# A two-layer transformer kernel on one core: row fetches through a ring of six buffers from the end of the first expert product on, and spills issued one at a time

## What is computed

```
def peer_ffn(h, w_q, sub_keys, u_tab, v_tab):      # cut; 16384 experts, 8 heads, 16 picks per head
    s = einsum(h @ w_q, sub_keys)                   # scores of 128 + 128 keys per head
    s_top, i_top = top_k(s, 16); best, pos = top_k(sums of pairs, 16)
    idx = ...; w = softmax(best)                    # 128 experts per position
    act = gelu(einsum('nhkd,nd->nhk', u_tab[idx], h))
    out = einsum('nhk,nhkd->nd', w * act, v_tab[idx])
```

## Time and profile before

| | |
|---|---|
| median of three runs | 3257.43 us |
| the profiled execution | 3261.52 us |
| its span | 3259.7 us |
| mean granted TensorE clock, share of full speed | 0.961 |
| busy: PE, DVE, ACT, POOL | 3080.0, 2214.2, 1151.3, 413.1 us |
| row 48 is used, row 79 is used | from 2576.11, from 2703.15 us |
| first matmul of the second product | 2707.39 us |

### The profile page before, as it was taken

How to read it: one execution, slowest core, us unless ns; L and a number is a source line. 1 busy time by engine, 2 the same in 40 slices (tenths; PEclk the granted TensorE clock), 3 DMA queues, 4 the chain that set the end, 5 groups by cost and what they waited for, 6 DMA issues and landing times.

```text
span 3259.7 us, 42988 instructions
## 1 busy us (share of the span) xinstructions
PE 3080.0 (94%) x17723; PEld 2817.2 (86%) x17723; DVE 2214.2 (68%) x3737; ACT 1151.3 (35%) x1569; POOL 413.1 (13%) x264
## 2 busy tenths in 40 slices
PE   7998998999999999999999998999999857999998
PEld 7888887878789889998878788899999857999998
DVE  6446875746644543666753579998997547899997
ACT  2234233222223432455552223444444312333332
POOL 0000000000000000000000000011111235566551
PEclk9888999999999998999999999999999978999999
DMA  5223112232232232211214414467477869999995
GB/s 227 106 97 137 44 49 103 83 104 92 84 122 73 71 142 101 78 65 66 99 64 161 181 65 177 164 217 256 169 243 261 294 223 363 402 401 401 402 401 219
DMA packets 215714, 571.10 MB, mean 175 GB/s; under 512 B 14288, under 2 KB 129488, under 8 KB 180064
## 3 DMA queue, kind: packets, MB, share of 16 engines
q1 hardware_dynamic: 176496, 426.14, 36.3%
q0 software_dynamic: 36864, 134.23, 11.0%
q10 hardware_dynamic: 2160, 7.99, 0.6%
HBM read 495.95 MB, written 72.35 MB: 174 GB/s over the span
## 4 chain that ended last, share of the span: by engine, by line
PE 78%; DVE 11%; DMA 5%; ACT 3%; SPq 2%; issue 1%; POOL 0%; DVEq 0%; ACTq 0%
PE bank L573 70%; DMA ub<-in_urow,gsel 3%; PE bank L1236 2%; DVE wl L528 2%; SPq L3046 2%; PE bank L637 1%; DMA gelu_spill<-gst 1%; DVE ub L3229 1%; PE bank L2507 1%; PE bank L585 1%; PE bank L644 1%; DVE Ah L3030 1%; ACT wh L521 1%; PE bank L2516 1%; PE bank L1501 0%
## 5 line engine op out<-in xcount | busy, mean ns | idle before, releaser
L573 PE MATMUL bank<-hh,wh 128*128 128x512 f32 (+2 forms) x2512 | 928.3, 370 | 70.6 <-DVE wl L528 60.6
L573 PE MATMUL bank<-hl,wh 128*128 128x512 f32 (+2 forms) x2512 | 902.2, 359 | 0.0
L573 PE MATMUL bank<-hh,wl 128*128 128x512 f32 (+2 forms) x2512 | 897.0, 357 | 0.0
L528 DVE TENSOR_TENSOR wl<-ring,wh 128x2048 fp32r<-128x2048 f32 (+2 forms) x249 | 554.1, 2225 | 312.6 <-ACT wh L521 311.9
L521 ACT ACTIVATE wh<-ring 128x2048 fp32r<-128x2048 f32 (+2 forms) x249 | 463.6, 1862 | 770.2 <-PE bank L573 761.6
L573 PEld LDWEIGHTS bank<-hh,wh 128*128 128x128 f32 x2512 | 487.4, 194 | 129.1 <-DVE wl L528 65.3
L573 PEld LDWEIGHTS bank<-hl,wh 128*128 128x128 f32 x2512 | 486.8, 194 | 50.4 <-issue 6.0
L573 PEld LDWEIGHTS bank<-hh,wl 128*128 128x128 f32 x2512 | 486.8, 194 | 46.4
L3215 POOL DMA_INDIRECT ub<-in_urow,gsel x128 | 193.6, 1513 | 1499.5 <-DVE gsel L2957 885.7
L573 PE MATMUL bank<-ph,wh 128*128 128x384 f32 x1024 | 346.1, 338 | 28.3 <-DVE pl L3178 28.3
L573 PE MATMUL bank<-ph,wl 128*128 128x384 f32 x1024 | 345.2, 337 | 0.0
(11 more groups left out here) (515 smaller groups left out, 4452.2 us busy)
## 6 DMA issues: line engine op xcount, KB each, us to landing
ring<-in_v SPq DMA_DIRECT2D x68, 1024.0 KB
ring<-in_u SPq DMA_DIRECT2D x64, 1024.0 KB
ring<-in_ada SPq DMA_DIRECT2D x24, 1024.0 KB
gelu_spill<-gst SPq DMA_DIRECT2D x128, 192.0 KB
weight_spill<-stage SPq DMA_DIRECT2D x24, 1024.0 KB, 11.1
gv<-gelu_spill SPq DMA_DIRECT2D x64, 384.0 KB
wv<-weight_spill SPq DMA_DIRECT2D x64, 384.0 KB
ring<-in_wup SPq DMA_DIRECT2D x22, 1024.0 KB
```

Of the source, the lines that this page charges most:

```text
L528: v.then_inc(v.e.tensor_tensor(wl[q % 2][:, 0:n], ring[k % 4][:, 0:n], wh[q % 2][:, 0:n].bitcast(F32), S_), s("parts"))
L573: ins = p.e.matmul(out, l, r, start=start and i == 0, stop=stop and i == len(pairs) - 1, skip_group_check=not check)
```

## The change

The ring. Rows 0 to 47 use the two buffers as before. From row `RT` = 48 on there are six: `ub2` to `ub5`, which now lie in the place of `x3` (over `stage0`), and the old two. Fetch 48 waits for the last spill of `stage0` (block 4), fetch n from 52 on waits until row n-6 is used. `ub6` and `ub7` are gone. The read of the residual into `x3` waits until all 256 rows are used. How many rows stand where does not change.

The spills. The four spills of a block are issued singly: those of the first block of a `hot(j)` at q = 16, 18, 20 and 22 of the same `hot(j)`; those of the second block in the first four steps of the next one; those of the last block (5) beside rows 48 to 51 (`rows_sy`).

```
         sb("ub_kept", [128, 2048], F32, ar)
         ph = [...]; pl = [...]
+        with ExitStack() as a2:
+            ub += [sb(f"ub{j}", [128, 1024], F32, a2) for j in range(2, 6)]
         x3 = sb("x3", [128, 8, 512], F32, ar)
         acc = sb("acc", [128, 1024], F32, ar)
         gwt = sb("gwt", [128, 128], F32, ar)
-        with ExitStack() as a2:
-            ub += [sb(f"ub{j}", [128, 1024], F32, a2) for j in range(2, 8)]
...
+    def spill(y, b, z):
+        y.wait_ge(s("stg"), 16 * b + 16)
+        y.e.dma_start(... block b, quarter z ...).then_inc(s(f"wst{b % 2}").sem, 16)
+
     def hot_sy(y, j):
-        for _ in range(5):
-            yield
-        for t, q in quads(j):
-            yield
-            if t % 16 == 15:
-                b = t // 16
-                y.wait_ge(s("stg"), t + 1)
-                for z in range(4):
-                    y.e.dma_start(... block b, quarter z ...)
+        for z in range(4):
+            yield
+            if j > 1:
+                spill(y, 2 * j - 3, z)
+        yield
+        for q in range(32):
+            yield
+            if q in (16, 18, 20, 22):
+                spill(y, 2 * j - 2, (q - 16) // 2)
         yield
...
+    def rows_sy(y, n0, n1):
+        for n in range(n0, n1):
+            if n0 == ROWS[3] and n - n0 < 4:
+                spill(y, 5, n - n0)
+            yield
...
-    RU = ROWS[-1]
+    RT, RU = ROWS[-2:]
     def ub_of(n):
-        return n % 2 if n < RU else (2, 3, 4, 5, 6, 7, 0, 1)[(n - RU) % 8]
+        return n % 2 if n < RT else (2, 3, 4, 5, 0, 1)[(n - RT) % 6]
...
-            if n == RU:
-                g.wait_ge(s("wst1"), WST[1])
-            if n < RU and n >= 2:
+            if n == RT:
+                g.wait_ge(s("wst0"), WST[0])
+            if n < RT and n >= 2:
                 g.wait_ge(s("gd"), n - 1)
-            elif n >= RU + 6:
-                g.wait_ge(s("gd"), n - 7)
+            elif n >= RT + 4:
+                g.wait_ge(s("gd"), n - 5)
...
+        y.wait_ge(s("gd"), 256)
         y.e.dma_start(x3[:, :, :], xd_).then_inc(s("x3").sem, 16)
```

More of the change, by code:

```diff
@@ L3035, in hot_ve @@
             yield
+    def spill(y, b, z):
+        y.wait_ge(s("stg"), 16 * b + 16)
+        y.e.dma_start(wd_[b, 16 * z:16 * z + 16].rearrange("s i x t -> i s (x t)"),
+                      stage[b % 2][:, 32 * z:32 * z + 32, :].rearrange("p (s x) t -> p s (x t)", x=2)
+                      ).then_inc(s(f"wst{b % 2}").sem, 16)
     def hot_sy(y, j):
-        for _ in range(5):
+        for z in range(4):
             yield
-        for t, q in quads(j):
+            if j > 1:
+                spill(y, 2 * j - 3, z)
+        yield
+        for q in range(32):
             yield
-            if t % 16 == 15:
-                b = t // 16
-                y.wait_ge(s("stg"), t + 1)
-                for z in range(4):
-                    y.e.dma_start(wd_[b, 16 * z:16 * z + 16].rearrange("s i x t -> i s (x t)"),
-                                  stage[b % 2][:, 32 * z:32 * z + 32, :].rearrange("p (s x) t -> p s (x t)", x=2)
-                                  ).then_inc(s(f"wst{b % 2}").sem, 16)
+            if q in (16, 18, 20, 22):
+                spill(y, 2 * j - 2, (q - 16) // 2)
         yield
@@ L3086, in choose_sy @@
     def choose_sy(y):
-        yield from choose(turn_idle(), lambda j: top_sy(y, j), lambda j: hot_sy(y, j), rows_idle, start_sy(y))
+        yield from choose(turn_idle(), lambda j: top_sy(y, j), lambda j: hot_sy(y, j), lambda m, n: rows_sy(y, m, n),
+                          start_sy(y))
     def u_pe(p):
```

## The result

The changed kernel takes 3214.14 us, the median of four runs (3211.01 to 3215.74), against 3258.38 us for the kernel before in the same comparison. The ratio is 0.9861, with a 95% interval of 0.9846 to 0.9876: 44 us faster. 3210 us was forecast, within 3188 to 3242 us. The profiled execution took 3215.74 us, its span is 3213.9 us, 45.8 us shorter than the span of before.

What follows compares the result with a forecast made beforehand. A two-buffer row-fetch loop was taken to bound rows 48 to 79, PE the second product. From 3261.5 us, ring 43, spills 3 and clock 1 came off: 3214.5 us, 3210 as median; 8 in 10 for 3188 to 3242 us.

Steps and rivals of the forecast that it cites:

- Six buffers for rows 48 to 79: Stage before the second product: removing the two-buffer loop cuts 131 us to 88, gain 43 us, bounds 35 to 58.
- 84 + 4: New stage length: 31.4 MB at 373 GB/s take 84 us, then 4 us from last row to first matmul.
- The bytes: Stage of rows 48 to 79: some 1 MB of 32.4 MB moves ahead of 2576 us, leaving 31.4 MB.
- Fetch 48's new wait costs nothing: Ring's start: block 4's last spill lands by 2551 us, fetch 47 left at 2561.6 us, 10 us to spare.
- Spread spills, 3 us: Spills issued singly delay gelu spills, ACT and PE less: 3 us gained, bounds 8 gained to 3 lost.
- PE's clock, 1 us: Second product's half-speed start costs 2.8 us; a shorter PE idle stretch before it gains 1 us, bounds 0 and 3.
- Six instead of eight in the second product, 0: Rows from 80 on: six buffers cost nothing, 0 us, bounds 2 us gained and 4 us lost.
- Rival C: Second product: six buffers too few if rows need over 11.9 us from issue to landing; slower, 3300 us at 15; chance 0.07.
- Rival A: Stage falls to PE's floor of 73 us with DMA at 402 GB/s: 3195 us, at best 3188; chance 0.14.
- Rival B: Stage: gelu spills behind 1 MB tiles in SP's queue become the wait, 99 us: 3221 to 3248 us; chance 0.22.
- Rival D: Fetch 48 finds `stage0` not free, ring fills late, or DVE meets the same landings: 3250 to 3262 us; chance 0.07.
- Sum: Whole kernel: 3261.5 - 43 - 3 - 1 = 3214.5 us for the profiled execution, so 3210 us as median.

Runs made afterwards that it cites:

- e1: The kernel after with spills issued as before, four in a row when a block is full; the ring of six stays: 3220.3 us, ratio 0.9889.
- e9: The kernel after with four instead of six buffers for rows 48 to 79, six from row 80 on: 3211.9 us, ratio 0.9857.
- e10: The kernel after with three instead of six buffers for rows 48 to 79: 3222.1 us, ratio 0.9885.
- e5: The kernel after with the second product's first three fetches of gelu and weights issued beside rows 70, 72 and 74, not behind row 79: 3206.9 us, ratio 0.9854.
- e2: The kernel before with only the spills spread as in the kernel after, row buffers as before: 3253.1 us, ratio 0.9985.
- e12: The kernel after, unchanged, measured again in a later comparison: 3214.6 us, ratio 0.9858.
- e4: The kernel after with four instead of six row buffers from row 80 on; rows 48 to 79 keep six: 3216.8 us, ratio 0.9886.
- e3: The kernel after with block 5's four spills beside rows 48, 54, 60 and 66 instead of 48 to 51: 3209.7 us, ratio 0.9857.
- e6: The kernel after with 24 instead of 16 rows beside the choice's last part, leaving 24 for the ring's stage: 3212.9 us, ratio 0.9867.
- e7: The kernel after with block 5's spills beside rows 48, 53, 58, 63 and the second product's first fetches beside 72, 74, 76: 3202.1 us, ratio 0.9835.
- e11: The kernel of e7 measured again, with more rounds, beside the unchanged kernel after: 3207.7 us, ratio 0.9838.
- e8: The kernel after with e6's row move, block 5's spills beside rows 56, 61, 66, 71, first fetches beside 76 to 78: 3212.2 us, ratio 0.9870.

## Why the prediction was right, and where it was off

- *Six buffers for rows 48 to 79:* gain 43 us forecast, 39.8 measured (from row 48 to the second product 131.3 and 91.5 us). The loop was named rightly (e1, e9 and e10 show it, and how it gives way between three and four buffers), and so was the next bound in the main: the rate of 373 GB/s, taken from the first 14 us of the old stage, was met, 373 up to the last row and 370 in the whole. The term that was off is "84 + 4": it was 80 + 12. Up to the last row 29.8 MB moved, not 31.4. Behind it came 12 us instead of 4, because I had put the tail (last gelu, spill, fetches, `weigh`) on PE's floor only. It was not hidden behind the rows: the second product starts 18.5 us after the last gelu, and `wv` shares the engines with rows and table tiles that nobody waits for yet. e5 takes 2.2 MB out of the way and gets 6 us.
- *The bytes:* a fall by 1 MB was forecast. From 9 us behind the last stage copy to the second product they rose from 33.4 MB (the line below, the kernel before) to 34.1. Three of block 5's four spills of 1 MB are issued inside the new stage, one inside the old, where the prediction has them compete as before. Fewer bytes up to the last row and a longer tail cancel in part, which is luck.

```profile
2575.54:2707.39 131.85, 65.82 (x309) 63.88 (x308) 58.03 (x79) 20.66 (x22) 51.91 (x37) 0.75 0.74 253
```

- *Fetch 48's new wait costs nothing:* right. It left at 2553.8 us, 0.3 us behind fetch 47; row 48 waited for nothing:

```profile
2552.58 0.94 POOL L3226 DMA_INDIRECT ub<-in_urow,gsel  x1 [3.98 <-DVE ub L3240]
2553.82 2.84 POOL L3226 DMA_INDIRECT ub<-in_urow,gsel  x1 [0.30 <-issue]
```

- *Spread spills, 3 us:* 6.6 us in the choice (e2), within the bounds of -3 to 8. The mechanism was right (a late gelu spill, ACT, then PE); the size was half. I priced PE's two largest gaps and wrote that nothing as large stood around the other blocks, but PE's waits over the whole choice fell by 5.9 us. One of the others, at 2297.5 us, was 1.34 us.
- *PE's clock, 1 us:* not shown. PE's wait before the second product shrank from 28.3 us (the prediction reads 26) to 20.5. In the first 42.6 us of the phase PE did 230 matmuls before, 234 in the kernel after, and 230 in its repetition e12. The whole phase took 1.0 us more, with a gap of 1.5 us (0.7 in e12, none before) behind a late `wv`. Beside 535.9 to 538.4 us over e1 to e12 (without e4) that is nothing.
- *Six instead of eight in the second product, 0:* right; e4 gives the margin, some 4 us in the landing of a row. Rival C would have needed landings of 13.5 us after the end of the issue, some 15.7 in the profile's count, where the longest is 11.6.
- *Rival A* (PE's floor of 73 us) fell: PE had 13.2 us of waits before its last step, and the share is 1.00 to 1.01. *Rival B*'s mechanism appeared, 34.1 us of ACT's waiting for gelu spills with 9.3 us of PE's behind it, and with it the hole in the DMA share, some 2 us. It does not set the whole length: in e3 these waits grow to 43.7 us and the stage shrinks. *Rival D* fell.
- *Sum:* the ring's gain was forecast 3 us too large, the spills' 4 us too small, the clock's 1 us too large. That these nearly cancel is part of the forecast's closeness (3210 for 3214).

## What to carry to other kernels

When a ring with too few buffers sets the pace, its replacement is bounded by the next full resource, and the old profile holds its price: divide all bytes of the stretch, the prefetches that nobody waits for yet included, by the rate of its fullest window. Put the chain that starts the next phase behind that, not beside it. Find the depth at which that resource is full (here four) before giving memory to more. Look at the share in short windows: an average of 1.01 held 8 us at 0.65 and 0.88. And price a stall by all waits of the engine over the stretch, not by its largest gaps: the two largest were 2.7 us, all of them 5.9, and the time lost 6.6.

## What was not expected of the hardware

With the DMA engines full, how long a transfer takes to land depends on its queue and on how much the other queue has under way. In the second product the medians from issue to landing are, with six row buffers and with four (e4), at 377 and 375 GB/s:

| us | six | four |
|---|---|---|
| row, through POOL | 9.7 | 8.5 |
| `gv`, SP's queue | 10.5 | 5.8 |
| `wv`, SP's queue | 14.7 | 7.7 |
| table tile, SP's queue | 17.1 | 10.8 |

The repetition e12 and e3, both with six, give the first column again within 1.4 us. So with the deeper ring SP's transfers landed later by 5 to 7 us at the same total rate, the rows by 1.2.

The rate at a share near 1 was not fixed: 366 to 375 GB/s for the stage in the kernel after, its repetition and e1, e4, e5, e6 and e9, 388 to 394 in e3, e7 and e11, 401 in the second product. The latter three have block 5's spills spread wide, but so has e8, at 374. A cause isn't shown.
